# When the second expert's weights and the next stage's rows are asked for in a two-layer backbone with routed experts

## The reference, cut to what matters

```python
def hier_moe(h, w_group, w_expert, w_gate, w_up, w_down):
    t = h.reshape(b * L, Dm)
    p_group = jax.nn.softmax((t @ w_group).astype(F32), axis=-1)
    p_top, g_idx = lax.top_k(p_group, 1)                       # 1 of 4 groups
    ...
    w_top, e_idx = lax.top_k(jax.nn.softmax(e_sel, axis=-1), TOP_K)   # 2 of its 4 experts
    w_top = w_top / jnp.sum(w_top, axis=-1, keepdims=True) * p_top
    ...
    for g in range(N_GROUPS):
        a = jnp.einsum('nd,edf->nef', t, w_gate[g])            # 1024 -> 256
        u = jnp.einsum('nd,edf->nef', t, w_up[g])
        hid = jax.nn.silu(a) * u * gates[:, g, :, None]
        out = out + jnp.einsum('nef,efd->nd', hid, w_down[g])  # 256 -> 1024
```

## Time and profile before

| | us |
|---|---|
| median of the three timed runs | 1861.51 |
| lowest and highest | 1859.23, 1861.71 |
| profiled execution, whole | 1862.22 |
| its span, from the first to the last instruction | 1860.4 |
| PE matmul busy | 1619.2 (87% of the span) |
| DVE, ACT, POOL busy | 820.8, 491.1, 259.5 |
| DMA: bytes moved, mean rate | 374.56 MB, 201 GB/s |

### The profile page before, as it was taken

The page is one execution under the profiler, slowest core; times in us unless marked ns, Lnnn a source line. Parts: engine busy times, 40 slices in busy tenths (PEclk is TensorE's granted clock), DMA queues, the critical chain, the costliest instruction groups (busy, mean ns, idle before and its releaser), DMA issues. The chain is left out here.

```text
span 1860.4 us, 17787 instructions
## 1 busy us (share of the span) xinstructions
PE 1619.2 (87%) x6305; PEld 978.9 (53%) x6305; DVE 820.8 (44%) x1349; ACT 491.1 (26%) x1001; POOL 259.5 (14%) x286
## 2 busy tenths in 40 slices
PE   4999989999979997999939999939959999399991
PEld 2566554444437775455527777614435545277770
DVE  2236556887706674553231111145456644411114
ACT  5122221001027774221101111133146631111112
POOL 0000000000024764111011000020000000110001
PEclk9999999999998999999959999969979999699996
DMA  8334535788847986531167999862040012679984
GB/s 310 135 125 142 160 129 194 280 288 291 273 134 221 303 262 244 197 120 50 45 267 289 355 353 350 301 239 73 0 93 1 1 69 91 249 252 345 350 316 158
DMA packets 168836, 374.56 MB, mean 201 GB/s; under 512 B 17698, under 2 KB 107106, under 8 KB 148802
## 3 DMA queue, kind: packets, MB, share of 16 engines
q1 hardware_dynamic: 144792, 287.22, 45.5%
q0 software_dynamic: 18608, 67.53, 9.7%
q10 hardware_dynamic: 5369, 18.95, 2.5%
HBM read 311.85 MB, written 61.82 MB: 201 GB/s over the span
## 5 line engine op out<-in xcount | busy, mean ns | idle before, releaser
L2027 PE MATMUL ex_ps_gu<-ex_wgu,ex_xT 128*128 128x256 f32 x1152 | 261.5, 386 | 11.5 <-DMA ex_wgu<-in_moe_w_gate_dram 7.9
L2027 PEld LDWEIGHTS ex_ps_gu<-ex_wgu,ex_xT 128*128 128x128 f32 x1152 | 220.9, 193 | 62.6 <-issue 24.2
L595 PE MATMUL ie_pu<-aT_even,ie_w_conv 128*128 128x512 f32 (+1 forms) x640 | 207.4, 486 | 0.0
L595 PEld LDWEIGHTS ie_pu<-aT_even,ie_w_conv 128*128 128x128 f32 x640 | 121.2, 190 | 84.6 <-issue 76.5
L1646 PE MATMUL po_ps_y<-po_w,po_yT 128*128 128x512 f32 x320 | 139.1, 592 | 2.0 <-DVE po_n L1545 2.0
L641 PE MATMUL ie_pu<-yacc_even,aT_even 128*128 128x512 f32 x288 | 127.4, 603 | 8.4 <-ACTq L745 8.4
L2045 PE MATMUL ex_ps_d<-ex_wd,ex_hT 128*128 128x512 f32 x288 | 131.2, 598 | 3.4 <-DVE ex_hT L2131 2.1
L641 PE MATMUL ie_pu<-hacc,aT_even 128*128 128x512 f32 x288 | 125.2, 593 | 0.0
L2127 DVE TENSOR_TENSOR ex_hid<-ex_hid,ex_ps_gu 128x256 f32<-128x256 f32 x36 | 15.2, 421 | 244.4 <-PE ex_ps_gu L2027 244.4
L1646 PEld LDWEIGHTS po_ps_y<-po_w,po_yT 128*128 128x128 f32 x320 | 60.0, 190 | 74.0 <-issue 71.7
L641 PEld LDWEIGHTS ie_pu<-yacc_even,aT_even 128*128 128x128 f32 x288 | 55.3, 193 | 78.8 <-issue 78.8
(11 more groups left out here) (455 smaller groups left out, 2387.7 us busy)
## 6 DMA issues: line engine op xcount, KB each, us to landing
ex_wgu<-in_moe_w_gate_dram SPq DMA_DIRECT2D x36, 1024.0 KB, 10.3
ex_wgu<-in_moe_w_up_dram SPq DMA_DIRECT2D x36, 1024.0 KB, 12.4
ex_wd<-in_moe_w_down_dram SPq DMA_DIRECT2D x36, 1024.0 KB, 8.9
ie_w_conv<-in_ada_w_dram SPq DMA_DIRECT2D x27, 1024.0 KB, 5.3
y<-ex_y ACTq DMA_DIRECT2D x36, 512.0 KB, 9.5
yacc_even<-in_ada_w_dram SPq DMA_DIRECT2D x13, 1024.0 KB, 5.2
room<-ac_rows SPq DMA_DIRECT2D x12, 1024.0 KB, 6.5
ie_w_conv<-in_ev_w_in_dram SPq DMA_DIRECT2D x10, 1024.0 KB, 5.9
```

The lines of the kernel that those rows point to most:

```text
L595: last = nc.tensor.matmul(pu[t][:, a:b], w_conv[h][:, k, t * P:(t + 1) * P], aT[:, k, a:b], start=(k == 0), stop=(k == KD - 1))
L2027: last = nc.tensor.matmul(ps_gu[s][part][:, 0:FF], xT[s][:, k, :], wgu[s][:, part, k, :], start=(k == 0), stop=(k == KD - 1))
```

## The change

SP asks for expert 0's weights alone in the routing block. The weights of expert 1 and the rows for the next stage move to the head of SP's list in the experts' block, behind a wait for both of the first two gathers. Nothing else changes, and no transfer is added or taken away.

```diff
@@ phase_route
         @block.sync
         def _(sp):
-            kit.load_experts(sp)
-            if layer == 0:
-                kit.load_odd_small(sp)
-            else:
-                kit.load_final(sp)
+            kit.load_whole(sp, 0)
@@ begin_experts
-    def load_first(sp):
-        for s in range(2):
-            for c in range(2):
-                load_gu(sp, s, s, c)
-            load_d(sp, s, s)
+    def load_whole(sp, s):
+        for c in range(2):
+            load_gu(sp, s, s, c)
+        load_d(sp, s, s)
@@ phase_experts, block.sync
+            for s in range(2):
+                sp.wait_ge(x_loaded[s], 16)
+            kit.load_whole(sp, 1)
+            if layer == 0:
+                kit.load_odd_small(sp)
+            else:
+                kit.load_final(sp)
             with sp.Fori(0, later_pairs(sp)) as i:
```

More of the change, by code:

```diff
@@ L1942, in gather_first @@
                                     in_offset=bass.IndirectOffsetOnAxis(ap=kit.slots_in[:, s:s + 1], axis=0)).then_inc(kit.x_loaded[s], 16)
-    kit.load_gu, kit.load_d, kit.load_experts, kit.gather_experts = load_gu, load_d, load_first, gather_first
+    kit.load_gu, kit.load_d, kit.load_whole, kit.gather_experts = load_gu, load_d, load_whole, gather_first
 def phase_experts(kit, layer, N):
```

## The result

The changed kernel takes 1851.49 us (median of 6 runs, 1849.88 to 1853.72). The kernel before took 1861.61 us in the same comparison (6 runs, 1859.23 to 1864.65). The ratio is 0.9944 with the 95% interval [0.9931, 0.9957]: by the ratio 10.4 us faster (10.1 between the medians), with the interval from 8.0 to 12.8. The forecast was 1853.0, a gain of 8.6.

A forecast was written before the change was run, and what follows sets the result against it. The second gather's landing, delayed by SP's traffic, was taken to bound each experts' block start. Gains of 4.1 and 4.5 us, all else 0, sum to 8.6: 1853.6 against the profiled time, 1852.9 against the median; predicted 1853.0, range 1849.8 to 1857.0.

The forecast's parts named there:

- What bounds the stretch: Before PE's first transpose in each layer's experts' block: POOL's second gather landing ends the stretch, 10.2 and 10.6 us after issue.
- Part 1: Before each layer's experts: without SP's traffic beside the gathers, 4.1 us gained in layer 0 and 4.5 in layer 1.
- Part 2: SP's two added waits in the experts' block ask for what POOL has already waited out: 0 us.
- Part 3: Moved requests, queued ahead of chunk 2's weights, are in before `gate_up(2)` needs them: cost 0, cover 2 to 3 us.
- Part 4: TensorE's clock rise, 8.0 us after PE's first transpose, moves along with the start: 0 us, 1.5 us per layer either way.
- Only the sharing goes: Rival at the gathers: they still begin late but no longer share, 3.6 us gained per layer, 1854.3 us; chance 0.15.
- Given back in the loop: Rival in the experts' loop: backlog makes `gate_up(3)` wait some 3.3 us per layer, 2.0 us gain left, 1859.5; chance 0.06.
- the gathers don't get faster: Rival at the gathers: their 10 us are POOL's or the block change's own, so time stays 1861.5 us; chance 0.04.
- the moved bytes starve chunk 2: Rival at `gate_up(2)`: at 250 GB/s the moved bytes come 9.3 and 10.7 us late, 1872.9 us; chance 0.04.

The follow-up runs named there:

- those of the wait: The changed kernel without SP's two waits, the moved requests staying at the head of SP's list in the experts' block: 1852.09 us, ratio 0.9953.
- each half: Two kernels, against the changed kernel: expert 1's weights back in the routing block, 1851.71 us; or the next stage's rows back there instead, 1852.42 us.

## Why the prediction was right

- **What bounds the stretch.** Right. The landing of the second gather sets S. Taking that gather out of the routing block brings S to 4.7 to 5.0 us behind the first. SP's transfers don't set it: `fn_x` lands 3.0 us behind S.
- **Part 1, the traffic goes: 4.1 and 4.5 us.** Right, a little small: 4.3 and 5.0. The quiet pair of rows 5 gave 6.03 and 5.89, and 0.1 to 0.2 us were added for PE's wait for ACT and DVE. The added share wasn't there: layer 0 reads 5.75 to 6.01 in six kernels (the changed one, and those of the wait, of each half, of layer 0 only, of the rows behind the loop), layer 1 5.62 to 5.88 in three.
- **Part 2, the wait: 0.** Right, shown by its removal. Where its condition is not met beforehand, with the second gather in the experts' block, the wait costs some 11 us (1857.5 against 1846.6) and not the 6.6 expected.
- **Part 3, the moved requests: 0.** The cost was right, the cover smaller than worked out. SP was through its list at S + 10.5 and asked for chunk 2's gate at S + 12.3. It landed in 11.7 us at 983.0, S + 24.0, and `gate_up(2)` began at S + 24.9. Predicted were S + 23.4 and S + 26.0. The bytes came as computed; the need came earlier, with the clock. Layer 1: 1641.06 against 1642.11. So 1 us of cover was left for the gate and not 2 to 3. For up, in at S + 26.8 and needed at S + 28.4, it was 1.6 us.
- **Part 4, the clock: 0, with 1.5 us per layer to either side.** The size was off within its bounds, and the assumption that rise and loss move along with the start didn't hold. In layer 0 the clock rises 5.7 us behind S instead of 8.0, and `gate_up(0)` takes 8.63 instead of 9.72 us (9.13 instead of 9.92 in layer 1). From S to `gate_up(2)` that gives 1.1 and 0.8 us. In layer 0 this goes with where S stands: S to `gate_up(1)` takes 13.24 to 13.38 us in all six kernels whose S comes 7.1 to 7.4 us behind the first gather, and 13.9 to 14.8 before and in the six others. In layer 1 no such order shows: 14.53 before, 13.74 after, but also 13.13 in the unchanged layer 1 of the kernel with layer 0 only. So layer 0's 1.1 us belong to the change as far as these runs tell, and layer 1's 0.8 stay open.
- **The loop.** Its 2.0 and 1.1 us in this execution were in no step. In layer 0 PE's waits for gate weights fell from the 4.5 us of rows 13 to 2.7. But the kernel with layer 0 only has the same lists there and waits 4.2 us:

```profile
PE ex_ps_gu L2029 <- DMA ex_wgu<-in_moe_w_gate_dram: 2.7, 6, 0.8
...
PE ex_ps_gu L2030 <- DMA ex_wgu<-in_moe_w_gate_dram: 4.2, 8, 0.9
```

Its loop takes 218.1 us, as before, and the changed kernel's 216.1 (the other experiments 214.7 to 217.7). So the same lists differ by 2 us between executions, and I don't put them down to the change.
- **The rivals.** *Only the sharing goes* is refuted as stated, since the first byte is the traffic's too, but it had the proportions right: most of the price is sharing. *Given back in the loop*, *the gathers don't get faster* and *the moved bytes starve chunk 2* didn't happen. In the changed kernel `gate_up(3)` of layer 0 waits 0.3 us and not the 3.3 of *given back in the loop*, whose 340 GB/s lies under all three rates of rows 7 and not only under the last two. Chunk 2 does starve when SP's list starts 5 us late, for 2.8 and 4.8 us and not the 9 to 11 of the rival.

What isn't settled: how the difference between 9.3 us (the two stretches) and 10.4 (the ratio) divides among layer 0's clock, layer 1's and the loop. The interval of 8.0 to 12.8 holds both numbers.

## What to carry to other kernels

In this kernel a change of block waits for the last gather that POOL has in flight, and not for SP's transfers. So look behind an idle first instruction for such a landing, issue before the change only the transfer that the very next instruction needs, and let the next one fly behind it. Ahead of such a small transfer ask in bulk only for what is through by then; it is the bytes still queued that count, and they do the same harm beside the last store that the next gathers wait for. An explicit wait on a queue's engine also holds all that is listed behind it: move the requests, and leave the wait away where their place already gives the order.

## What the runs showed of the hardware

- **The change of block waits for POOL's gathers in flight and not for SP's transfers.** S comes 0.6 us behind the landing of the last gather in the kernel before, while `fn_x` of SP lands 3.0 us behind S.
- **A gather's first byte waits while another queue has work.** It comes 1.8 us behind the issue into quiet engines, 3.8 us where 1.05 MB stood in q1, and 4.3 to 4.9 behind more. With 1.05 MB ahead, q0 moved 3 packets in 4.1 us. Why is open; larger backlogs gave no larger delay.
- **Queues share by packet.** Packets of 7.6 KB against 3.8 KB left the gathers 33% of the engines, packets of 3.6 KB about half.
- **SP can be held at a small request.** The first norm weight row (32 KB) took 7.66 us to ask for the earlier trace rows and 5.37 after the change, where a 1024 KB load takes 0.3 to 1.5 us. It isn't the row itself: with no expert weights just ahead of it in the list (the kernel with expert 1's weights early) the same request took 0.52 us. What holds SP is open.

```profile
960.65 0.52 SPq L2311 DMA_DIRECT2D io_wn_row<-in_od_q_norm_w_dram  x1
```

- **Short stretches at half clock in mid work.** They last a little over 3 us and cost about 1.6 us each. Between the two experts' stages they come at the same two places of the program, in some executions and not in others. Another came right behind PE's waits of 2.8 and 4.8 us for weights. Why they come is open.
